# Attention with the next head's operands split in thirds on ScalarE and VectorE, and all six score groups shifted by VectorE

## What is computed

```
s = jnp.einsum('bqhd,bkhd->bhqk', qblk, k).astype(jnp.float32) * scale
p = jax.nn.softmax(s, axis=-1).astype(v.dtype)
return jnp.einsum('bhqk,bkhd->bqhd', p, v)
```

## Time and profile before

| what | value |
|---|---|
| median of three runs | 3417.44 us |
| lowest and highest | 3409.56 and 3417.75 us |
| the profiled execution, its time | 3412.3 us |
| the profiled execution, span of the trace | 3410.5 us |
| mean granted TensorE clock | 0.941 of full |
| busy: TensorE, VectorE, ScalarE, GpSimd | 3076.6, 1947.3, 1375.1, 648.5 us |
| attention: from its first DMA to its last reciprocal | 1094.3 to 2114.6 us of the span |

### The profile page before, as it was taken

How to read it: one execution, slowest core, us unless ns; L and a number is a source line. 1 busy time by engine, 2 the same in 40 slices (tenths; PEclk the granted TensorE clock), 3 DMA queues, 4 the chain that set the end, 5 groups by cost and what they waited for, 6 DMA issues and landing times. The chain is left out here.

```text
span 3410.5 us, 43961 instructions
## 1 busy us (share of the span) xinstructions
PE 3076.6 (90%) x14693; PEld 2177.3 (64%) x14693; DVE 1947.3 (57%) x2632; ACT 1375.1 (40%) x2061; POOL 648.5 (19%) x459
## 2 busy tenths in 40 slices
PE   6799999999886899999999997998399999999992
PEld 1355555555586565565565563777298989989892
DVE  1133333333475677777777775444766666766663
ACT  0133333333222655666566664211244444444432
POOL 0011111111254233223322321211011111101011
PEclk9899999999877899999999998999599999999996
DMA  8521121111223110110110101332366667676656
GB/s 320 149 70 61 62 68 61 61 61 55 99 82 80 23 24 12 32 32 5 31 32 5 32 5 55 139 108 105 122 198 208 211 205 229 203 216 201 212 159 234
DMA packets 254709, 363.74 MB, mean 107 GB/s; under 512 B 36436, under 2 KB 170583, under 8 KB 252888
## 3 DMA queue, kind: packets, MB, share of 16 engines
q1 hardware_dynamic: 245336, 327.97, 30.0%
q0 software_dynamic: 9216, 33.56, 4.4%
HBM read 279.65 MB, written 81.83 MB: 106 GB/s over the span
## 5 line engine op out<-in xcount | busy, mean ns | idle before, releaser
L467 PE MATMUL bank<-w_in_sb,h_T 128*128 128x512 f32 (+1 forms) x1440 | 609.3, 578 | 2.1 <-DVE h_T L616 2.1
L1643 PE MATMUL ebank<-gathered_T,w_gate_up 128*128 128x256 f32 x4608 | 555.6, 282 | 3.5 <-DVE gathered_T L1836 1.7
L1643 PEld LDWEIGHTS ebank<-gathered_T,w_gate_up 128*128 128x128 f32 x4608 | 550.9, 189 | 7.5 <-issue 6.3
L1077 PE MATMUL abank<-scores,head_v 128*128 128x512 f32 x1152 | 546.2, 602 | 2.2 <-ACT scores L1115 2.2
L1040 PE MATMUL abank<-head_qT,head_kT 96*128 96x512 f32 x1728 | 504.8, 437 | 24.5 <-POOL head_qT L1019 24.5
L467 PEld LDWEIGHTS bank<-w_in_sb,h_T 128*128 128x128 f32 x1440 | 270.1, 191 | 299.0 <-issue 298.8
L1040 PEld LDWEIGHTS abank<-head_qT,head_kT 96*128 96x128 f32 x1728 | 327.5, 190 | 172.1 <-issue 96.1
L1103 ACT ACTIVATE scores<-abank 128x512 f32<-128x512 f32 x576 | 314.3, 608 | 77.0 <-PE abank L1040 71.2
L1077 PEld LDWEIGHTS abank<-scores,head_v 128*128 128x128 f32 x1152 | 218.3, 194 | 180.7 <-issue 163.2
L1026 POOL TENSOR_TENSOR scores<-scores,max_for_pool 128x1536 f32<-128x1536 f32 x64 | 220.9, 3474 | 571.3 <-ACT max_for_pool L1109 571.3
L1115 ACT ACTIVATE scores<-scores 128x1536 f32<-128x1536 f32 x192 | 287.4, 1498 | 40.0 <-DVE scores L1157 35.6
(11 more groups left out here) (258 smaller groups left out, 3470.2 us busy)
## 6 DMA issues: line engine op xcount, KB each, us to landing
w_gate_up_whole<-in_w_exp_gate SPq DMA_DIRECT2D x48, 1024.0 KB, 5.4
w_gate_up_whole<-in_w_exp_up SPq DMA_DIRECT2D x48, 1024.0 KB, 8.0
w_down_whole<-in_w_exp_down SPq DMA_DIRECT2D x192, 256.0 KB, 3.6
ada_w<-in_w_ada SPq DMA_DIRECT2D x12, 2048.0 KB, 12.6
scratch_ret<-ret_rows SPq DMA_DIRECT2D x72, 256.0 KB, 2.5
x_tile<-in_x_all SPq DMA_DIRECT2D x18, 512.0 KB
w_in_sb<-in_w_in SPq DMA_DIRECT2D x4, 2048.0 KB, 18.8
chunk_qk<-scratch_ret SPq DMA_DIRECT2D x16, 512.0 KB
```

Source lines behind the costliest of these rows:

```text
L467: m = pe.matmul(banks[bank][:, 0:n], hT[u][:, k, :], w_in[:, k, lo:lo + n], start=(k == 0), stop=(k == KD - 1))
L1077: m = pe.matmul(banks[5 + j % 2][:, :], v1[u][:, kt, :], sc[j % 2][:, kt, :], start=(kt == 0), stop=(kt == T - 1))
L1643: x = pe.matmul(banks[f % 3][:, j * CAP:(j + 1) * CAP], w_gu[c][:, wp, j, k, o:o + P], xsT[:, xp, k, :], start=(k == 0 and n == 0), stop=( ...
```

## The change

The split of the next head is cut into three thirds of 768 columns (of the query operand's 2048 columns 768, 768 and 512), made at `j` = 0, 1, 2 and `j` = 4, 5, 6 instead of at once at 1 and 5. ScalarE rounds a third at the end of its turn, VectorE subtracts it at the end of its own, behind `output`. GpSimd has nothing left in the loop. VectorE shifts groups 2 to 5 at the start of a turn, where it shifted 2 and 3. The second spread into bank 7, `copy_max` and the buffer `ms` go. The loads count on two semaphores, one for key and query and one for the value; the split waits only for the first. For head 0 the split is made in the same thirds, with all subtractions on VectorE, and TensorE scores before the value has landed. The stage `modulation` clears its semaphores at its end (an instruction on GpSimd) and is followed by an empty block, which is one more barrier of all engines.

```
+@contextmanager
+def stage_semaphores(nc):
...
+    yield sem
+    nc.clear_and_free_semaphores(taken)
+    with nc.Block():
+        pass
...
-    with ExitStack() as ctx:
+    with stage_semaphores(nc) as sem, ExitStack() as ctx:
...
-        ms = sb("max_for_pool", [P, QB])
...
-        kv_loaded = ParitySignal(nc, ctx, "head_kv_loaded", 4)
+        kq_loaded, v_loaded = ParitySignal(nc, ctx, "head_kq_loaded", 3), ParitySignal(nc, ctx, "head_v_loaded")
...
+        THIRD = TOK // 3
+
+        def thirds(u, n):
+
+            c = slice(n * THIRD, (n + 1) * THIRD)
+            return (kT[u], k_whole[u], c), (qT[u], q_whole[u], slice(c.start, min(c.stop, SEQ)))
+
         def split_next(split, pair, j):
 
-            if j == 1:
-                split(pair * 2 + 1, 1)
-            if j == 5 and not (isinstance(pair, int) and pair == H // 2 - 1):
-                split(pair * 2 + 2, 0)
+            if j < 3:
+                split(pair * 2 + 1, 1, j)
+            if 4 <= j < 7 and not (isinstance(pair, int) and pair == H // 2 - 1):
+                split(pair * 2 + 2, 0, j - 4)
...
-            def turn(pair, j, b, more):
-                s = sc[j % 2]
-                for g in range(4, GROUPS):
-                    x = s[:, g * G:(g + 1) * G, :]
-                    sg["max_copied"].wait(pool, b)
-                    pool.tensor_tensor(x, x, mid(ms[:, :], G), ALU.subtract).then_inc(sg["shifted_pool"].sem, 1)
-                split_next(split, pair, j)
...
-                for bank, user in ((4, "shifted"), (7, "max_copied")):
-                    sg[user].wait(pe, b - 1)
-                    for c in range(4):
-                        m = pe.transpose(banks[bank][:, c * P:(c + 1) * P], mrep[:, c, :], perm["ident"][:, :])
-                    m.then_inc(sg["max_psum"].sem, 1)
+                sg["shifted"].wait(pe, b - 1)
+                for c in range(4):
+                    m = pe.transpose(banks[4][:, c * P:(c + 1) * P], mrep[:, c, :], perm["ident"][:, :])
+                m.then_inc(sg["max_psum"].sem, 1)
...
-            pe.wait_ge(ones_set, 2)
-            head_ready(0, 0)
+            sg["rounded"].wait(pe, 0)
+            sg["rest"].wait(pe, 0)
...
+            pe.wait_ge(ones_set, 2)
+            v_loaded.wait(pe, 0, 0)
             loop(pe, turn)
...
+            def split(head, u, n):
+
+                kq_loaded.wait(act, head, u)
+                for x, whole, c in thirds(u, n):
+                    act.activation(x[:, 0, c], whole[:, 1, c], ACT.Copy).then_inc(sg["rounded"].sem, 1)
...
-                if more:
-                    copy_max(b + 1)
...
+            def split(head, u, n):
+
+                for i, (x, whole, c) in enumerate(thirds(u, n)):
+                    sg["rounded"].wait(dve, head, 2 * n + i + 1)
+                    dve.tensor_tensor(x[:, 1, c], whole[:, 1, c], x[:, 0, c].bitcast(F32), ALU.subtract).then_inc(sg["rest"].sem, 1)
...
             def turn(pair, j, b, more):
-                for g in (2, 3):
+                for g in range(2, GROUPS):
                     shift(j, b, g)
...
                 output(j, b)
+                split_next(split, pair, j)
```

More of the change, by code:

```diff
@@ L3 @@
 from concourse import mybir
-from contextlib import ExitStack
+from contextlib import ExitStack, contextmanager
 F32 = mybir.dt.float32
@@ L116, in split_tensor, with sem @@
     return parts, whole
+@contextmanager
+def stage_semaphores(nc):
+    taken = []
+    def sem(name):
+        taken.append(nc.alloc_semaphore(name=name))
+        return taken[-1]
+    yield sem
+    nc.clear_and_free_semaphores(taken)
+    with nc.Block():
+        pass
 def mid(ap, n):
@@ L989, in load @@
             def load(head, u):
[L990 to L994, removed]
+                for dst, src, loaded in ((k_whole[u][0:NOPE, 1, :], scratch["kT_heads"][bass.ds(head, 1), :, :].rearrange("o d n -> (o d) n"), kq_loaded),
+                                 (k_whole[u][NOPE:DQ, 1, :], scratch["krT"], kq_loaded),
+                                 (q_whole[u][:, 1, :], scratch["qT"][bass.ds(head, 1), :, CTX:].rearrange("o d n -> (o d) n"), kq_loaded),
+                                 (v1[u][:, :, 0:DV], scratch["v"].rearrange("(t p) (h d) -> p t h d", p=P, h=H)[:, :, bass.ds(head, 1), :].rearrange("p t o d -> p t (o d)"), v_loaded)):
+                    sp.dma_start(dst, src).then_inc(loaded.sems[u], 32)
             load(0, 0)
@@ L1012, in _ @@
                 pool.memset(v1[u][:, :, DV:], 1.0).then_inc(ones_set, 1)
[L1014 to L1019, removed]
-            def turn(pair, j, b, more):
-                s = sc[j % 2]
-                for g in range(4, GROUPS):
-                    x = s[:, g * G:(g + 1) * G, :]
-                    sg["max_copied"].wait(pool, b)
-                    pool.tensor_tensor(x, x, mid(ms[:, :], G), ALU.subtract).then_inc(sg["shifted_pool"].sem, 1)
-                split_next(split, pair, j)
-            split(0, 0, parts=(1,))
-            loop(pool, turn)
         @block.tensor
@@ L1043, in head_ready @@
             def head_ready(head, u):
-                kv_loaded.wait(pe, head, u)
+                kq_loaded.wait(pe, head, u)
+                v_loaded.wait(pe, head, u)
                 sg["rounded"].wait(pe, head)
@@ L1103, in copy_scores @@
                     act.activation(sc[j % 2][:, kt, :], banks[kt % 3][:, :], ACT.Copy).then_inc(sg["scores"].sem, 1)
[L1105 to L1109, removed]
             def turn(pair, j, b, more):
@@ L1113, in turn @@
                     x = sc[j % 2][:, g * G:(g + 1) * G, :]
-                    sg["shifted"].wait(act, b, g + 1) if g < 4 else sg["shifted_pool"].wait(act, b, g - 3)
+                    sg["shifted"].wait(act, b, g + 1)
                     act.activation(x, x, ACT.Exp, scale=ATT_SCALE).then_inc(sg["probs"].sem, 1)
@@ L1120, in turn @@
                 split_next(split, pair, j)
-                if more:
-                    copy_max(b + 1)
-            split(0, 0)
+            for n in range(3):
+                split(0, 0, n)
             for g in range(GROUPS):
                 copy_scores(0, 0, g)
-            copy_max(0)
             loop(act, turn)
@@ L1155, in shift @@
                 x = sc[j % 2][:, g * G:(g + 1) * G, :]
-                sg["max_psum"].wait(dve, b, 1)
+                sg["max_psum"].wait(dve, b)
                 dve.tensor_tensor(x, x, mid(banks[4][:, :], G), ALU.subtract).then_inc(sg["shifted"].sem, 1)
@@ L1176, in turn @@
                 output(j, b)
-            sg["rounded"].wait(dve, 0, 1)
-            dve.tensor_tensor(kT[0][:, 1, :], k_whole[0][:, 1, :], kT[0][:, 0, :].bitcast(F32), ALU.subtract).then_inc(sg["rest"].sem, 1)
+                split_next(split, pair, j)
+            for n in range(3):
+                split(0, 0, n)
             for g in range(1, GROUPS):
@@ L1185, in _ @@
             loop(dve, turn)
-ATTENTION_STEPS = {"rounded": 2, "rest": 2, "s_psum": 18, "scores": 18, "max_keys": 7, "max_T": 1, "max_rep": 2,
-                   "max_psum": 2, "shifted": 4, "shifted_pool": 2, "max_copied": 1, "probs": 6, "out_psum": 1, "out": 2, "out_stored": 1}
+ATTENTION_STEPS = {"rounded": 6, "rest": 6, "s_psum": 18, "scores": 18, "max_keys": 7, "max_T": 1, "max_rep": 2,
+                   "max_psum": 1, "shifted": 6, "probs": 6, "out_psum": 1, "out": 2, "out_stored": 1}
 ATTENTION_DMAS = ("out_stored",)
```

2 lines of the change are left out of this document (removed).

## The result

The changed kernel takes 3442.44 us (median of four runs, 3440.48 to 3449.36) against 3415.8 us for the kernel before in the same comparison: 26.6 us or 0.85% more, ratio 1.0085 with an interval from 1.0065 to 1.0104. It is slower.

What follows compares the result with a forecast made beforehand. TensorE was taken to bound the ordinary turn (29.17 us), with VectorE close behind in a ring of waits. The terms - 44.8 + 25.7 + 41.4 + 10.5 - 6.6 + 1 gave + 27 us, forecast 3441 us, range 3420 to 3465.

Steps and rivals of the forecast that it cites:

- Part 1: Attention, GpSimd's split removed: VectorE's folds and copies run at once, seven long turns lose 6.40 us each, gain 44.8 us.
- The rival that ScalarE's rounding holds VectorE: Long turns: something other than GpSimd holds the fold; with all 44.8 us staying, 3486 us; chance 0.04.
- Part 2: Shifts of groups 4 and 5 on VectorE, four transposes fewer: ordinary turn stays at 29.17 us, between 28.7 and 29.5.
- The ring: Attention turn: reciprocal, shifts, maxima, transposes, value product, reciprocal; forecast 29.16 us, with VectorE's slack used up.
- the lower bound that I gave as 28.7: Ordinary attention turn: TensorE's own work, 28.7 us, if the maxima were back to back sooner.
- Part 3: Split thirds on VectorE behind the output delay shift 2: 14 turns of 31.0 us, + 25.7 us over ordinary ones.
- Part 4: Turns 3 and 7: TensorE idles about 6.35 us for the last third; turn 35.1 us, + 41.4 us, clock extra.
- the clock: Head's turns: TensorE runs slowly behind its wait, 1.5 us a head, + 10.5 us in all, bounds 0 to 24.
- Part 5: Attention's start: rounding no longer waits for the value's DMA, gain 6.6 us, bounds 3 and 8.
- My sign, first scores at about 1112: Attention's start, trace after: TensorE's first scores at about 1112, against 1117.89 before.
- Part 6: Modulation's end: second barrier and semaphore clear cost + 1 us, bounds 0 and 4.
- slack of some 3 us: VectorE in an ordinary attention turn: some 3 us of slack, all ahead of maxima that wait for data.

Runs made afterwards that it cites:

- the shifts alone: Kernel before with only the shifts of groups 4 and 5 moved to VectorE, no second spread or maximum copy; split whole on GpSimd: 3452.0 us, ratio 1.0095.
- with the ring open: Changed kernel with a block's output in VectorE's next turn, third behind group 1's shift, head load waiting for the value product: 3388.5 us, ratio 0.9904.
- the fourth kernel: Changed kernel with the third's key subtraction behind the spread copy and its query subtraction behind group 1's shift: 3360.8 us, ratio 0.9833.
- padding: Changed kernel without semaphore clearing, plus four or sixteen one-column VectorE memsets in modulation: 3443.5 us (ratio 1.0077) and 3447.3 us (1.0075).
- the experiment with GpSimd's shifts: The fourth kernel with groups 4 and 5 shifted by GpSimd again, second spread and `copy_max` back: 3384.0 us, ratio 0.9897.
- ahead of the output: Changed kernel with the third of the split ahead of VectorE's output instead of behind it: 3376.3 us, ratio 0.9872.

## Why the prediction was right

I forecast 27 us more; it is 26.6. That the two agree to half a microsecond is luck: read one by one from the two traces, the thirty turns cost 37.8 us more (forecast 32.8), the start gives 7.2 and the stage's end costs 0.5, together + 31. The stages that no edit touches differ by more than those 4 us from one trace to the next. What the traces bear out is the mechanism of each part and its size within a few us. By its steps, against the kernel after:

- **Part 1, 44.8 us gained.** The seven long turns are gone, no pair of folds takes over 1.42 us. That GpSimd's subtractions caused them is borne out from the other side by the shifts alone, where the hold grew with the order of arrival. The rival that ScalarE's rounding holds VectorE is not borne out: beside it the fourth and fifth maximum, with two inputs in SBUF, run at full speed in the kernel after (four in 7.14 us). The rule from the Trainium skill (SBUF — State Buffer, Who interferes with whom), two SBUF inputs against a GpSimd instruction that reads SBUF, agrees with the held third (2.05 us) and the unslowed shifts.
- **Part 2, nothing.** Ordinary turns 29.18 against 29.17, in the kernel after and with the shifts alone. The ring is real: with it opened the turn is 28.73, the lower bound that I gave as 28.7. TensorE's busy time does not tell the two apart: it is 29.17 us in an ordinary turn of the kernel before, 29.17 in one of the fourth kernel with four transposes fewer, and 28.73 with the ring open, all of the turn each time. In the last pair of heads, straight code, turns are 29.36, 0.2 more than worked out.
- **Part 3, + 25.7.** The turns behind a third are 30.91 us, in the last pair 31.1, against 31.0 forecast; 14 x 1.74 = 24.4. The two kernels that move the third into idle time of VectorE give back 66 and 81 us together with part 4.
- **Part 4, + 41.4 and + 10.5 for the clock.** Head's turns are 36.6 to 38.1, on average 37.4 against 36.6. The wait is 5.93 us (6.35 forecast), and TensorE's first score stands 5.80 us behind the reciprocal (5.65 forecast). From there to the transposes of the head's turn shown are 23.3 us instead of 21.3, of which the slow matmuls make 1.9 (nine scores 4.20 instead of 2.63, two value matmuls 1.38 instead of 1.02). On the average of seven heads 2.3 us are left over the 35.1 worked out, where I had 1.5 for the clock: 5 to 6 us in all, inside my bounds. This is the one term that was undersized.
- **Part 5, - 6.6.** From the first DMA of the attention to the first reciprocal: 1171.19 - 1101.31 = 69.9 against 1171.38 - 1094.28 = 77.1, so 7.2 us. ScalarE starts 10.4 us behind the first DMA instead of 14.3, and the first scores 16.4 instead of 23.6. My sign, first scores at about 1112, did not come as it stood: they are at 1117.7, since the attention itself began 7.0 us later (below).
- **Part 6, + 1.** The distance of the stages is 1.86 instead of 1.33 us: 0.5. That was only the visible price. Without the same edit the changed kernel is some 20 us slower, by the two stops. I had no such term, and that it came out at nothing was luck: of the programs without padding, five had stops at the loop's turn and seven, the kernels before and after among them, had none. With them the time would have been near 3462, still in the range, but for a reason that the prediction doesn't have.

The profiled execution, 3449.4 us, is 7 us above the other three (3440.5 to 3442.5). In its trace the attention's first DMA is 7.0 us later than before (1101.31 against 1094.28), of which 0.9 was there at the start of the retention stage and 6 came within it, where the change touches nothing. This hides the gain of part 5 in the traces' totals. The first reciprocal moves as much between two programs whose stages ahead of it differ by twelve memsets: 1164.1 with four, 1171.8 with sixteen.

What I had wrong without it counting: VectorE's idle time ahead of its maxima I called slack of some 3 us. It is slack for two more shifts, which stand behind shift 2, but not for anything ahead of shift 2, since that delays ScalarE's exponential and its copies. In part 3 I had this right, in the experiment with GpSimd's shifts I forgot it.

## What to carry to other kernels

Find the ring of waits that closes every turn of a loop, and put new work of an engine where it waits for another inside that ring, not where it has just handed on: the same subtractions cost 81 us at one place and nothing at the other. What an engine will wait for must be complete before the work queued ahead of that wait runs out, or its last piece stands in series with everything. TensorE waited not at all with the third in the gaps, 0.88 us with it ahead of the output and 5.93 us with it behind. And a gap at a loop's turn that no row explains may be the program's layout; add a few instructions and look again before believing that an edit costs or gains 20 us.

## What the runs showed of the hardware that was not expected

- VectorE stopped for 8.6 us at the turn of a loop body, at both backward jumps of the three passes, in some programs and not in others that differ by four tiny instructions far ahead; 4.7 us when SyncE's bulk load came behind the jump. Programs with stops move 29 packets of 8 KB on an instruction queue in the attention, those without 17 to 20. What exactly VectorE waits for is open.
- VectorE and GpSimd alternate where both have instructions queued that exclude one another: a fold waits for one subtraction of GpSimd and is let in before the next, so the price is a whole foreign instruction for each of one's own (10.32 us for two folds), and 0.3 us of difference in arrival decides between one and two.
- TensorE behind an idle stretch of 5.93 us ran at 1.2 GHz: nine score matmuls took 4.20 us instead of 2.63. Behind 3.04 us it did so in part (granted clock 0.77 over 4 us), behind 0.88 us it did not (nine in 2.33).
